# Q and K projections with tokens stationary and weights moving, and transposes of their blocks in the last round of a decoder trunk

## What is computed

```python
mod = (cond @ mod_w[i] + mod_b[i])[:, None, :]
sh_m, sc_m, g_m, sh_f, sc_f, g_f = jnp.split(mod, N_MOD, axis=-1)
h = x * (1.0 + sc_m) + sh_m
qkv = h @ w_qkv                      # 256x2048 @ 2048x6144
q, k, v = jnp.split(qkv, 3, axis=-1)
z = jnp.einsum('bqhd,bkhd->bhqk', qb, kb) * HEAD_DIM ** -0.5   # 16 heads of 128
...                                  # a from z: log-sigmoids, a reverse cumulative sum, exp
y = jnp.einsum('bhqk,bkhd->bqhd', a, vb) @ w_o
x = layer_norm(DEEPNORM_ALPHA * x + (1.0 + g_m) * y, ln_g[i, 0], ln_b[i, 0])
```

## Time and profile before

| | |
|---|---|
| median of 3 runs | 2220.59 us (2220.35 to 2221.53) |
| the profiled execution's own time | 2218.09 us |
| its span, first to last instruction | 2216.2 us |
| PE busy | 2176.3 us, 98% |
| weight loads (PEld) busy | 1832.1 us, 83% |
| DVE busy | 1758.6 us, 79% |
| ACT busy | 1127.6 us, 51% |
| HBM read | 623.15 MB, 282 GB/s over the span |

### The profile page before, as it was taken

How to read it: one execution, slowest core, us unless ns; L and a number is a source line. 1 busy time by engine, 2 the same in 40 slices (tenths; PEclk the granted TensorE clock), 3 DMA queues, 4 the chain that set the end, 5 groups by cost and what they waited for, 6 DMA issues and landing times.

```text
span 2216.2 us, 27554 instructions
## 1 busy us (share of the span) xinstructions
PE 2176.3 (98%) x10446; PEld 1832.1 (83%) x10446; DVE 1758.6 (79%) x1804; ACT 1127.6 (51%) x1403; POOL 7.1 (0%) x25
## 2 busy tenths in 40 slices
PE   5999999999999999999999999999999999999998
PEld 5999988888888888888878888888888888888886
DVE  7899999977988988999988898667666666655667
ACT  4777875365345435435455433337544543543552
POOL 0000000000000000000000000000000000000000
PEclk9999999999999999999999999999999999999999
DMA  9999998869999999999958988766787787866672
GB/s 353 385 386 396 398 376 300 283 231 351 394 347 325 370 341 321 360 344 335 335 175 295 332 295 286 235 205 212 255 295 232 249 277 231 265 212 190 203 265 100
DMA packets 317043, 650.41 MB, mean 293 GB/s; under 512 B 31840, under 2 KB 63088, under 8 KB 315248
## 3 DMA queue, kind: packets, MB, share of 16 engines
q1 hardware_dynamic: 313568, 634.73, 83.2%
q10 hardware_dynamic: 3344, 13.93, 1.6%
HBM read 623.15 MB, written 2.12 MB: 282 GB/s over the span
## 4 chain that ended last, share of the span: by engine, by line
PE 87%; DVE 6%; DMA 3%; issue 2%; ACT 1%; SPq 1%; ACTq 0%; DVEq 0%
PE bank L1439 25%; PE bank L1440 25%; PE bank L1441 25%; PE bank L1429 3%; PE bank L1432 3%; PE bank L1431 3%; DMA mod_raw<-in_mod_w 2%; DVE mod_acc L984 1%; DVE w_low L1069 1%; PE bank L1447 1%; PE bank L1451 1%; PE bank L1446 1%; DMA stage<-stage 1%; DMA raw<-in_attn_w_qkv 0%; SPq L559 0%
## 5 line engine op out<-in xcount | busy, mean ns | idle before, releaser
L719 ACT ACTIVATE w_high<-raw 128x1024 fp32r<-128x1024 f32 x752 | 788.0, 1059 | 966.2 <-PE bank L1441 910.7
L1069 DVE TENSOR_TENSOR w_low<-raw,w_high 128x1024 fp32r<-128x1024 f32 x752 | 912.5, 1222 | 354.8 <-ACT w_high L719 353.6
L1439 PE MATMUL bank<-w_high,h_high 128*128 128x512 f32 x1632 | 636.5, 390 | 3.0 <-DVE w_low L1069 3.0
L1440 PE MATMUL bank<-w_low,h_high 128*128 128x512 f32 x1632 | 635.0, 389 | 0.0
L1441 PE MATMUL bank<-w_high,h_low 128*128 128x512 f32 x1632 | 635.0, 389 | 0.0
L984 DVE SCALAR_TENSOR_TENSOR mod_acc<-mod_raw,cond,mod_acc 128x1024 f32<-128x1024 f32 x345 | 442.2, 1282 | 23.5 <-DMA mod_raw<-in_mod_w 20.6
L1439 PE MATMUL bank<-w_high,hid_high 128*128 128x512 f32 x1048 | 408.1, 389 | 2.3 <-DVE w_low L1069 2.3
L1441 PE MATMUL bank<-w_high,hid_low 128*128 128x512 f32 x1048 | 407.7, 389 | 0.0
L1440 PE MATMUL bank<-w_low,hid_high 128*128 128x512 f32 x1048 | 407.7, 389 | 0.0
L1439 PEld LDWEIGHTS bank<-w_high,h_high 128*128 128x128 f32 x1632 | 306.4, 188 | 68.2 <-issue 3.8
L1441 PEld LDWEIGHTS bank<-w_high,h_low 128*128 128x128 f32 x1632 | 306.4, 188 | 63.7
(11 more groups left out here) (156 smaller groups left out, 1176.6 us busy)
## 6 DMA issues: line engine op xcount, KB each, us to landing
raw<-in_mlp_w SPq DMA_DIRECT2D x512, 512.0 KB, 5.7
mod_raw<-in_mod_w SPq DMA_DIRECT2D x368, 512.0 KB, 8.2
raw<-in_attn_w_qkv SPq DMA_DIRECT2D x96, 512.0 KB, 10.6
raw<-in_conv_w_in SPq DMA_DIRECT2D x96, 512.0 KB, 5.7
stage<-stage SPq DMA_DIRECT2D x176, 128.0 KB, 2.9
raw<-in_attn_w_o SPq DMA_DIRECT2D x32, 512.0 KB, 8.2
raw<-in_conv_w_out SPq DMA_DIRECT2D x32, 512.0 KB, 4.7
mod_raw<-in_mod_w SPq DMA_DIRECT2D x32, 256.0 KB, 6.5
```

Source lines behind the costliest of these rows:

```text
L719: act.activation(chunk_slots(n)[0], raw[:, n % NCH], ACT.Copy).then_inc(high_done, 1)
L1069: dve.tensor_tensor(low_, raw[:, n % NCH], high.bitcast(F32), ALU.subtract).then_inc(raw_used, 1)
L1439: pe.matmul(dst, high[:, k, c], wh, start=first, stop=False, skip_group_check=True)
L1440: pe.matmul(dst, high[:, k, c], wl, start=False, stop=False, skip_group_check=True)
```

## The change

Q and K are now formed as V is, by `token_row`: `feature_row` is gone, and a chunk of Q or K takes 12 matmuls with 512 moving columns. The sums of a visit are then rows of tokens. `take_out` and `put_back` keep them in the place of `q_t` or `k_t`, block by block: four blocks of 128 tokens x 128 features for each half of the tokens. In the last round PE turns the blocks (`turn_qk`): four transposes into bank 6 for one half of the tokens of one group, behind each of the chunks 74 to 89, the first half behind the chunk after the group's last one and the second half behind the next. ACT copies the turned blocks over the old ones (`take_turned`), five steps later in its program. A turn waits until the group has been taken out (`parts_out`) and, as there is one bank for it, until the turn before it has been copied (`qk_out`). The scores of heads 0 and 1 wait for the turned blocks, and those of head 1 move from chunk 89 to chunk 90.

```diff
@@ -91,6 +91,9 @@
     QC = QKV * PART_CH
     BANK0 = N_VISITS - W_O
 
+    QK_VISITS = [N_VISITS - QKV + g for g in range(QK)]
+    QK_TURN_AT = {LAST_CHUNK[v] + 1 + t: (g, t) for g, v in enumerate(QK_VISITS) for t in range(TT)}
+
     def goes_on(v):
         return LEADING <= v < 2 * LEADING or QKV + LEADING <= v < N_VISITS
     MODT = UNITS * KT
@@ -157,7 +160,7 @@
 
     HEAD_TILES = {s: 1 for s in range(3, 16) if s != 13} | {16: 2, 17: 2, 18: 2, 19: 2}
     N_HEAD_TILES = sum(HEAD_TILES.values())
-    SCORES_AT = {N_O - 10: 0, N_O - 7: 1, N_O - 2: 2}
+    SCORES_AT = {N_O - 10: 0, N_O - 6: 1, N_O - 2: 2}
     SOFT_AT = {N_O - 5: 0, N_O - 1: 1, N_O + SLOTS - 1: 2}
     SOFTPLUS_AT = {N_O - 3: 0, N_O - 1: 1, N_O + 2: 2}
     HEADS_BLOCK, HEADS_SUM, HEADS_WRITE = 8, 12, 13
@@ -305,6 +308,7 @@
             return bank[4], bank[1 if b == HEADS_BLOCK else 7]
 
         c_ps = bank[5][:, 0:KT]
+        qk_ps = bank[6]
 
         def start_ps(v):
             return bank[2 * (v % 2)], bank[2 * (v % 2) + 1]
@@ -340,6 +344,8 @@
         chunk_mult = sem("chunk_mult")
         banks_free = sem("banks_free")
         parts_out = sem("parts_out")
+        qk_turned = sem("qk_turned")
+        qk_out = sem("qk_out")
         post_done = sem("post_done")
         half_mult = sem("half_mult")
         swapped = sem("swapped")
@@ -745,8 +751,9 @@
                 if g >= QK:
                     rows = v_tok[:, :, cols(g - QK)]
                     return [(start_ps(v)[t][:, :], rows[:, t, :]) for t in range(TT)]
-                rows = flat((q_t, k_t)[g // NG][:, g % NG * GT:(g % NG + 1) * GT, :])
-                return [(start_ps(v)[b][:, :], rows[:, b * 2 * T:(b + 1) * 2 * T]) for b in range(2)]
+                rows = (q_t, k_t)[g // NG][:, g % NG * GT:(g % NG + 1) * GT, :]
+                return [(start_ps(v)[t][:, :].rearrange("p (m n) -> p m n", m=GT), rows[:, :, toks(t)])
+                        for t in range(TT)]
 
             def take_out(v):
 
@@ -756,6 +763,12 @@
                     ins = act.activation(dst, src, ACT.Copy,
                                          scale=ZSCALE if r == QUARTERS - 1 and g < NG else 1.0)
                 ins.then_inc(parts_out if goes_on(v + 2) else banks_free, 1)
+
+            def take_turned(g, t):
+
+                act.wait_ge(qk_turned, TT * g + t + 1)
+                act.activation((q_t, k_t)[g // NG][:, g % NG * GT:(g % NG + 1) * GT, toks(t)],
+                               qk_ps[:, :].rearrange("p (m n) -> p m n", m=GT), ACT.Copy).then_inc(qk_out, 1)
 
             def put_back(v):
 
@@ -789,6 +802,8 @@
                     soft_log(SOFT_AT[n])
                     if SOFT_AT[n] == LEAD - 1:
                         attend(0)
+                if n - SLOTS - 1 in QK_TURN_AT:
+                    take_turned(*QK_TURN_AT[n - SLOTS - 1])
                 if n in visit_at:
                     v = visit_at[n]
                     take_out(v)
@@ -1421,17 +1436,15 @@
 
             turn_x(0)
 
-            def feature_row(dsts, k, wh, wl, first, last):
-
+            def turn_qk(g, t):
+
+                pe.wait_ge(parts_out, sum(goes_on(u) for u in range(2, QK_VISITS[g] + 3)))
+                if g or t:
+                    pe.wait_ge(qk_out, TT * g + t)
                 for m in range(GT):
-                    c = slice(m * P, (m + 1) * P)
-                    dst = dsts[m // 2][:, T * (m % 2):T * (m % 2 + 1)]
-                    pe.matmul(dst, wh[:, c], h_high[:, k, :], start=first and m % 2 == 0, stop=False,
-                              skip_group_check=True)
-                    pe.matmul(dst, wh[:, c], h_low[:, k, :], start=False, stop=False, skip_group_check=True)
-                    ins = pe.matmul(dst, wl[:, c], h_high[:, k, :], start=False, stop=last,
-                                    skip_group_check=True)
-                return ins
+                    rows = (q_t, k_t)[g // NG][:, g % NG * GT + m, toks(t)]
+                    ins = pe.transpose(qk_ps[:, m * P:(m + 1) * P], rows, ident[:])
+                ins.then_inc(qk_turned, 1)
 
             def token_row(par, t, k, wh, wl, high, low, first, last):
 
@@ -1484,6 +1497,8 @@
                     pe.wait_ge(mod_reduced, 2 * reduced(HEADS_BLOCK))
                 elif s >= 4:
                     pe.wait_ge(att_a, s - 3)
+                elif s < LEAD - 1:
+                    pe.wait_ge(qk_out, TT * QK if s else TT * (NG + 1))
                 pe.matmul(z[:, 0:T], k_t[:, s, 0:P], q_t[:, s, :], start=True, stop=False,
                           skip_group_check=True)
                 pe.matmul(z[:, T:ZC], k_t[:, s, P:T], q_t[:, s, P:T], start=False, stop=False,
@@ -1526,13 +1541,12 @@
                     k = CK * jj + kk
                     pe.wait_ge(h0_done, k + 1 if r == 0 and jj == 0 else H0_PIECES[r + 1])
                     begins, ends = r == 0 and k == 0, k == GT - 1
-                    if g < QK:
-                        ins = feature_row(start_ps(v), r * GT + k, wh[:, kk, :], wl[:, kk, :], begins, ends)
-                    else:
-                        for t in range(TT):
-                            ins = token_row(v % 2, t, r * GT + k, wh[:, kk, :], wl[:, kk, :], h_high, h_low,
-                                            begins, ends)
+                    for t in range(TT):
+                        ins = token_row(v % 2, t, r * GT + k, wh[:, kk, :], wl[:, kk, :], h_high, h_low,
+                                        begins, ends)
                 ins.then_inc(chunk_mult, 1)
+                if n in QK_TURN_AT:
+                    turn_qk(*QK_TURN_AT[n])
                 if n == LEADING - 2:
                     sum_mod(1)
                 sum_after(n)
```

## The result

| | before | after |
|---|---|---|
| median of 6 runs, us | 2220.48 (2220.08 to 2221.53) | 2229.62 (2227.78 to 2231.80) |
| median when both ran again on another chip, us | 2218.97 (21 runs) | 2229.52 (5 runs) |
| profiled execution, us (its span) | 2218.09 (2216.2) | 2231.80 (2230.1) |
| last matmul of chunk 95 starts, us | 315.51 | 326.02 |

The changed kernel is slower: 1.0042 times the time before (1.0032 to 1.0052), and 1.0046 (1.0034 to 1.0059) in the second comparison. By the medians that is 9.1 and 10.6 us; 2233.1 was forecast, the range was 2225 to 2239.

A forecast was written before the change was run, and what follows sets the result against it. DVE's low parts and tile loads were taken to pace the projection, with PE just behind. Terms -0.1 - 2.2 + 7.0 + 6.8 + 1.0 = +12.5 us on 2220.59 gave 2233.1 us, range 2225 to 2239.

The forecast's parts named there:

- what is left at chunk 74: Start of chunk 74, last round: of the first three rounds' 7.7 us matmul gain, only -0.1 us remains.
- 14 chunks of the last round: Chunks 74 to 87: token rows save 0.16 us a chunk on PE, -2.2 us.
- 64 transposes in 16 turns: Last round on PE: 64 transposes at 0.109 us each, covered by nothing, +7.0 us.
- seven waits for the late copy: Last round, turns (1, 0) to (7, 0): PE waits for ACT's copy, 0.97 us a pair, +6.8 us.
- the scores of head 1: Behind chunk 90: these scores wait for the last copy of a turned block, +1.0 us.
- The low parts pace rounds 1 to 3: DVE's low parts and tile loads form a loop, 2.70 us a step, so PE can't use 7.7 us there.
- The rate of a 512-wide matmul: Q and K chunks: token rows start 0.2265 us apart, so a chunk takes 2.72 us where it took 2.88.
- Rival E: Turns in the last round: short groups of transposes don't overlap, 10.5 us more, 2243.6 us; chance 0.06.
- The delay goes through whole: Behind chunk 95: the heads start later and stay as long, so all +12.5 us reach the end.
- C, the other side: PE paces all four rounds, `low(72)` ends 7.7 us earlier; without waits -3.2 us, 2217.4; chance 0.07.
- D: PE paces all four rounds, but turns wait for the copy: +4.8 us, 2225.4; chance 0.08.
- B: Last round: the turns don't wait, the copy comes free sooner: +4.7 us, 2225.3; chance 0.12.

The follow-up runs named there:

- after_again: The changed kernel run once more, unaltered, beside the kernel before on another chip: 2229.52 us, 1.0046 times before.
- e2: Changed kernel without the turns, their copies and the waits for them (scores read blocks in the wrong layout): 2218.84 us, 0.9998 times before.
- e3: Changed kernel with feature rows kept for Q and K, but with turns, copies and waits: 2233.76 us, 1.0059 times before.
- e5: Kernel before with modulation tiles 16 and up, as far as chunk 95, loaded by half: 2220.78 us, 1.0006 times before.
- e6: Changed kernel with modulation tiles 16 and up, as far as chunk 95, loaded by half: 2225.10 us, 1.0019 times before.
- e1: Changed kernel with ACT's copy of a turned block four steps behind its turn in place of five: 2223.09 us, 1.0014 times before.
- e4: Changed kernel with the second turns of groups 0 to 5 put into a second bank, bank 5: 2225.46 us, 1.0028 times before.
- e8: Kernel before with six second modulation tiles moved from chunks 42 to 71 to chunks 73 to 88, block sums later: 2225.56 us, 1.0026 times before.

## Why the prediction came out right

By its own steps, against the first trace of before; in brackets against the second, with after_again.

| step | forecast | measured |
|---|---|---|
| what is left at chunk 74 (its first matmul) | -0.1 | -2.0 (-0.6) |
| 14 chunks of the last round | -2.2 | -2.2, by the pitch of the matmuls |
| 64 transposes in 16 turns | +7.0 | 16 x 0.49 = +7.8 |
| seven waits for the late copy | +6.8 | 7 x 0.85 = +6.0 |
| the scores of head 1 | +1.0 | +0.8 |
| chunk 95 | +12.5 | +10.5 (+11.7) |

The measured steps add up to 10.4 and 11.8.

**The low parts pace rounds 1 to 3: right for the changed kernel**, and the step that was mis-sized stands on it. "What is left at chunk 74 is -0.1 us" took the low parts of the traced execution as fixed. They came 1.8 us earlier. Of that, 1.0 lies between two traces of the same kernel: the second trace of before has `low(72)` at 241.45 (last section). The token-row kernels with full loads and the table of before have it between 240.65 and 241.43. What is left for the change is 0 to 0.8 us, small as forecast. The expected sign "`low(72)` near 242.4" was too sharp for one execution. The mechanism itself is shown by e2, e3, e5 and e6: token rows bring 0 to 2 us alone, and in rounds 2 and 3 all of their 5.1 us once the loads are halved. One half of the account was too simple: "none of it waits for PE" holds for DVE, but ACT does wait there for PE before it takes out Q and K, 28.6 us from 103 to 243, and `high` stands behind these rows in its order. The waits of ACT before:

```profile
ACT k_t L756 <- PE bank L1432: 15.2, 8, 3.3
ACT q_t L756 <- PE bank L1432: 13.4, 8, 2.4
```

With feature rows PE's own work and the loop take the same time (e5), so that in the kernel before neither alone sets the pace.

**The waits: right**, by place (L1446, seven times, and L1502), by cause (e1 removes all of them, e4 the five it was made for) and by pitch (7.27 for 7.29). The price apiece was forecast at 0.97 and is 7.27 - 6.42 = 0.85 (6.42 is two chunks and two turns at 3.21; e1 shows 6.41), since the pair without a wait is longer than I took it.

**The transposes: 0.49 a turn for 0.44.** This is the term that was too small, 7.8 us in place of 7.0. The two errors, in the turns and in the price of a wait, cancel in a waiting pair: there the time of the copy rules, which was forecast nearly to the point. So it is not to the credit of the two prices that their sum is 13.8 us in the forecast and as measured. The Trainium skill's 275 ns apiece (TensorE: Matmul & The Clock Gate, Part 4: PE-mode transpose) would be, as an estimate, 1.1 us a turn; here it is the duration of one (272 ns in the middle of the 32 of `q_t`) and not the pitch, also in groups of four. Rival E falls with it.

**The rate of a 512-wide matmul: right.** 12 matmuls take 2.72 us in the changed kernel, as the token rows of V did. The Trainium skill's formula (same page, Back-to-back issue gap), which that section gives for matmuls in isolation, has 216 ns and hardly a gain (0.03 us a chunk); the Q and K chunks now show 0.2265.

**The delay goes through whole: right** (10.5 at chunk 95, 10.3 at 121 and at 144). The medians say 9.1 and 10.6. Forecast minus result is 3.5 us: 2.0 from the table, the other 1.5 lies between the trace and the medians. Part of that is the clock. On the chip of after_again the kernel before took 2217.6 us on average in ten executions with a mean granted clock of 1.000 and 2222.6 in five with 0.997. Four of each kernel at 0.999 are 10.8 apart (2219.5 and 2230.3). So a difference of medians also counts how often each kernel met a lower clock, and the forecast laid a full-clock trace and a median side by side. For the six runs of before in the first comparison the clock is on record for the profiled one alone, so how much of the 1.5 it makes there stays open.

C, the other side, and with it D, which took C's pace, fell by e2 and by where `low(72)` ends. B needed turns that don't wait: e1 shows what it would have been, +4.1 us where +4.7 was forecast.

## What to carry to other kernels

A full PE does not prove that PE sets the pace: two loops of nearly equal pace look the same, and the one behind shows only in when its products come (here the low parts, 0.2 us ahead of PE at the start of a round) and in an experiment that lightens it. Lighten it in both kernels: in the kernel before alone it changed nothing. When results go through one bank, place the engine that empties it first in that engine's own program: one step earlier on ACT was worth 6.4 us here, more than a second bank for six of the groups (4.5). And before trading one layout for another that must be turned back, hold the turns (7.8 us) against the part of the gain that falls where the engine is the bound (2.2 us here), not against all of it (10.2).

## What the runs showed of the chip that was not expected

**A short stretch at half clock.** In the second trace of before, windows on both sides of 1122.3 us:

```profile
1118.90:1122.30 3.40, 3.40 (x8) 2.72 (x9) 3.23 (x3) 0.00 (x0) 0.00 (x0) 0.50 0.64 158
1122.30:1125.70 3.40, 3.40 (x16) 2.73 (x16) 1.04 (x1) 1.06 (x1) 0.00 (x0) 1.00 0.74 198
```

and what PE did ahead of it:

```profile
1118.86 0.75 PE L1439 MATMUL bank<-w_high,hid_high 128*128 128x512 f32 x1 [2.30 <-DVE w_low L1069]
```

The granted clock is 0.50, so 1.2 GHz, behind a wait of 2.30 us, and 8 matmuls start where 16 do at 2.4 GHz: about 1.7 us lost. The changed kernel has the same at another time:

```profile
1132.60:1135.90 3.30, 3.30 (x9) 2.53 (x9) 1.86 (x2) 0.34 (x1) 0.00 (x0) 0.50 0.66 174
```

The first trace of before, e4 and e6 do not have it, though the same wait stands in each of them. In the first trace of before, where the granted clock stays at 1.00 behind it:

```profile
1120.03 0.47 PE L1439 MATMUL bank<-w_high,hid_high 128*128 128x512 f32 x1 [2.31 <-DVE w_low L1069]
```

So the wait belongs to the program, and the fall of the clock to the execution. It is also why the profiled execution of after is so long: 10.3 us behind that of before at chunk 144, 12.1 at chunk 432, and 13.9 at the end, with the stretch at 1132.6 us between the first two and another at 2221.4 to 2224.8 between the last two. e8 has one more, at 264.7 to 268.1 us behind the wait of 1.82 us: 15 matmuls 0.214 apart where 0.12 is the pace, 1.4 us. e5 and e8 have one in the first round too. The Trainium skill (TensorE: Matmul & The Clock Gate, HAM oscillation — how this bites in real kernels) tells of such a fall of the clock behind waits for DMA, and these traces agree in kind; the waits here were for DVE. Seven waits of 0.7 us ahead of turns in the last round of after did not lower the clock, and neither did the 2.57 us in round 1 of the first trace of before: it is 1.00 there.

**Two traces of one kernel differ by 1 us at a place.** In the first trace of before a wait in round 1 is longer (2.57 us, ending at 41.93, where the second trace has 1.78, ending at 40.56). With 0.6 us that it was behind already, its PE is 1.4 us behind from chunk 4 on, 1.2 at chunk 71, 1.0 at chunk 95 (315.51 against 314.48). In round 3 one tile comes late as well: `low(53)` ends at 185.33 and not at 183.20. That puts the low parts 2.1 us behind for one chunk and does not add to PE's lateness. So terms smaller than 1 us can't be read from one trace of each kernel here. What made the wait of round 1 longer was not tried.
